# Moving the hidden chunk's send and turn behind each pair's third group, and a fast group's second ring slot ahead of its sums, in a streaming-encoder block

## The reference

```python
D_MODEL, SEQ, D_FF = 2048, 256, 5632

def rmsnorm(x, g):
    return x * rsqrt(mean(x * x, axis=-1) + EPS) * g

def swiglu(x, w_in, w_out):
    gate, up = split(x @ w_in, 2, axis=-1)      # w_in: 2048 x 11264
    return (silu(gate) * up) @ w_out            # w_out: 5632 x 2048

h = x + 0.5 * swiglu(rmsnorm(x, ffn1_norm), ffn1_w_in, ffn1_w_out)
h = h + mixer(h)
h = h + cross_attention(h, mem)
h = h + 0.5 * swiglu(rmsnorm(h, ffn2_norm), ffn2_w_in, ffn2_w_out)
out = rmsnorm(h, final_norm)
```

## Time and profile before

| | |
|---|---|
| median of 3 runs (lowest to highest) | 2130.85 us (2129.96 to 2134.89) |
| the profiled execution, and its span | 2129.56 us, 2127.5 us |
| PE busy | 2106.6 us (99%) |
| DVE busy | 1534.0 us (72%) |
| ACT busy | 1089.3 us (51%) |
| HBM traffic | 222 GB/s over the span |

### The profile page before, as it was taken

One profiled execution on the slowest core, in us unless ns is written; L12 is line 12 of the kernel. 1 busy time (PEld: TensorE's weight loads), 2 busy tenths in 40 slices (PEclk: granted clock), 3 DMA queues, 4 the chain that ended last, 5 costly groups with the idle time before them and its releaser, 6 DMA issues.

```text
span 2127.5 us, 27271 instructions
## 1 busy us (share of the span) xinstructions
PE 2106.6 (99%) x9405; PEld 1740.4 (82%) x9405; DVE 1534.0 (72%) x1647; ACT 1089.3 (51%) x1249; POOL 38.4 (2%) x50
## 2 busy tenths in 40 slices
PE   9999999999999999999999999999999999999998
PEld 7788888888888888888888888887887888888887
DVE  7999999984555576566565656569999999964444
ACT  6555555553444455456544545455555555543433
POOL 0000000000000031000000000000000000000000
PEclk9999999999999999999999999999999999999999
DMA  7676667776666676765587766575667767775554
GB/s 278 223 231 218 221 231 228 226 245 239 208 228 214 220 265 218 237 213 184 178 285 239 237 208 191 189 247 198 229 226 223 224 217 221 225 287 195 190 188 157
DMA packets 185317, 472.37 MB, mean 222 GB/s; under 512 B 17056, under 2 KB 67616, under 8 KB 185120
## 3 DMA queue, kind: packets, MB, share of 16 engines
q1 hardware_dynamic: 183088, 464.11, 66.1%
q0 software_dynamic: 1728, 6.82, 0.9%
q10 hardware_dynamic: 432, 0.53, 0.1%
HBM read 443.60 MB, written 27.79 MB: 222 GB/s over the span
## 4 chain that ended last, share of the span: by engine, by line
PE 60%; DVE 18%; DMA 11%; issue 8%; ACT 2%; DVEq 0%; SPq 0%; ACTq 0%; POOLq 0%; POOL 0%
PE acc L1869 18%; PE acc L1871 18%; PE acc L1872 18%; DMA raw<-in_ffn_w_in 11%; DVE w_lo L1186 9%; DVE t_raw L1312 2%; DVE raw L1310 2%; DVE t_raw L1309 2%; DVE stage L1293 1%; PE acc L1893 1%; PE acc L1892 1%; PE acc L1894 1%; DVE stage L1226 1%; ACT w_hi L727 1%; DVE shared L1348 0%
## 5 line engine op out<-in xcount | busy, mean ns | idle before, releaser
L1186 DVE TENSOR_TENSOR w_lo<-raw,w_hi 128x1024 fp32r<-128x1024 f32 x765 | 924.8, 1223 | 477.1 <-ACT w_hi L727 474.9
L727 ACT ACTIVATE w_hi<-raw 128x1024 fp32r<-128x1024 f32 x765 | 796.8, 1056 | 857.5 <-PE acc L1872 532.7
L1869 PE MATMUL acc<-w_hi,a_hi 128*128 128x512 f32 x744 | 290.3, 390 | 0.5 <-DVE w_lo L1186 0.5
L1872 PE MATMUL acc<-w_hi,a_lo 128*128 128x512 f32 x744 | 289.6, 389 | 0.0
L1871 PE MATMUL acc<-w_lo,a_hi 128*128 128x512 f32 x744 | 289.5, 389 | 0.0
L1869 PE MATMUL acc<-w_hi,b_hi 128*128 128x512 f32 x576 | 225.6, 392 | 0.0
L1871 PE MATMUL acc<-w_lo,b_hi 128*128 128x512 f32 x576 | 224.3, 389 | 0.0
L1872 PE MATMUL acc<-w_hi,b_lo 128*128 128x512 f32 x576 | 224.2, 389 | 0.0
L1892 PE MATMUL acc<-w_hi,a_hi 128*128 128x512 f32 x460 | 179.0, 389 | 0.0
L1893 PE MATMUL acc<-w_lo,a_hi 128*128 128x512 f32 x460 | 179.0, 389 | 0.0
L1892 PE MATMUL acc<-w_hi,b_hi 128*128 128x512 f32 x460 | 179.0, 389 | 0.0
(11 more groups left out here) (273 smaller groups left out, 2645.1 us busy)
## 6 DMA issues: line engine op xcount, KB each, us to landing
raw<-in_ffn_w_in SPq DMA_DIRECT2D x349, 512.0 KB, 4.2
raw<-in_ffn_w_out SPq DMA_DIRECT2D x176, 512.0 KB, 4.3
raw<-in_w_mix_in SPq DMA_DIRECT2D x80, 512.0 KB, 4.4
raw<-in_w_ckv SPq DMA_DIRECT2D x64, 512.0 KB, 4.3
memq<-bounce SPq DMA_DIRECT2D x196, 128.0 KB, 4.3
bounce<-stage SPq DMA_DIRECT2D x37, 512.0 KB, 3.1
raw<-in_w_mix_out SPq DMA_DIRECT2D x32, 512.0 KB, 4.5
raw<-in_w_cq SPq DMA_DIRECT2D x32, 512.0 KB, 4.3
```

Source lines behind the costliest of these rows:

```text
L727: eng.activation(w_hi[:, u % RING], raw[:, u % RING], ACT.Copy).then_inc(w_hi_done, 1)
L1186: eng.tensor_tensor(w_lo[:, u % RING], raw[:, u % RING], w_hi[:, u % RING].bitcast(f32), ALU.subtract).then_inc(w_lo_done, 1)
L1869: eng.matmul(dst, x_hi[:, rows], w_hi[:, slot, i], start=start and i == 0, stop=False)
L1872: last = eng.matmul(dst, x_lo[:, rows], w_hi[:, slot, i], start=False, stop=stop and i == UK - 1)
```

## The change

- `SEND_AT` goes from 7 to 12 and `FETCH_AT` from 10 to 14. On DVE `hidden` moves from behind place 3 to behind place 7, `turn` from behind the third group's `t_lo_part` to behind place 12, and `fill_lo` from behind place 10 to behind the first add of the gate sums. ACT's `fill_hi` moves from between places 10 and 11 to behind `copy_p1`. DVE gains a wait on its own `t_read` ahead of writing the gate to `stage`.
- TensorE does the two products of a group's second ring place ahead of the three with summed weights. The semaphore `t_used` goes: `w_used` of the second place now says that as well.
- The first pair's mixed blocks move to places 5, 7, 9 (FFN1) and 9, 11, 13 (FFN2). ACT runs a one-element Silu at place 14 (FFN1) and 6 (FFN2), so the table it needs is loaded there.

```diff
-SEND_AT = 7
-MIX_AT = [10, 12, 14][-FAST:]
-FETCH_AT = 10
+SEND_AT = 12
+FETCH_AT = 14
+X_MIX_AT = [5, 7, 9]
+H3_MIX_AT = [9, 11, 13]
...
@@ ACT, fast_hi and pair @@
                     if s:
-                        eng.wait_ge(t_used, fast_count(base, j, s))
+                        eng.wait_ge(w_used, base + PAIR * j + FAST_AT[s - 1] + 2)
...
-                        if s == FAST - 1:
-                            fill_hi(turned, number(TURNS, hid) + j, hid_dst, src=stage4)
                         split(base, j, FAST_AT[s] + 3, PAIR)
                     for p in range(4 * FAST, PAIR - 3):
                         split(base, j, p, PAIR)
                     eng.wait_ge(w_used, base + PAIR * j + FAST_END)
                     eng.activation(copy_p1, sum_p1, ACT.Copy).then_inc(p1_copied, 1)
+                    fill_hi(turned, number(TURNS, hid) + j, hid_dst, src=stage4)
...
@@ ACT, first pair (FFN1; FFN2 the same at p == 6) @@
+                    if p == 14:
+                        eng.activation(first_exp[:], ones[:, 0:1], ACT.Silu)
-                    if p - 1 in MIX_AT:
-                        s = MIX_AT.index(p - 1)
+                    if p - 1 in X_MIX_AT:
+                        s = X_MIX_AT.index(p - 1)
...
@@ DVE, pair @@
                     for s in range(FAST):
                         fast_lo(j, s)
-                        if s == FAST - 1:
-                            turn(number(TURNS, hid) - 1 + j, stage4)
                         unit_lo(j, FAST_AT[s] + 2)
                         if s == 0:
                             up_drained(j - 1)
-                        if s == FAST - 1:
-                            fill_lo(split_number(hid) - 1 + j, lo, hi, src=stage4)
                         unit_lo(j, FAST_AT[s] + 3)
-                        if s == 0:
+                        if s == 1:
                             hidden(j - 1)
                     for p in range(4 * FAST, PAIR - 3):
                         unit_lo(j, p)
+                    turn(number(TURNS, hid) - 1 + j, stage4)
                     eng.wait_ge(p1_copied, done)
                     eng.tensor_tensor(shared[:, 0], sum_p6, copy_p1, ALU.add).then_inc(p6_added, 1)
+                    fill_lo(split_number(hid) - 1 + j, lo, hi, src=stage4)
                     unit_lo(j, PAIR - 3)
...
+                    eng.wait_ge(t_read, number(FILLS, hid) + j)
                     eng.tensor_tensor(stage[:, 0], acc[:, 0], copy_p1, ALU.add)
...
@@ DVE, behind the first pair @@
-                mix_parts_lo(base, MIX_AT.index(PAIR - 2), *mixed)
...
@@ TensorE, fast @@
-                    eng.wait_ge(t_lo_done, fast_count(base, j, s) + 1)
-                    three(sum_p7, s3, sum_block(0), start, stop)
-                    three(sum_p6, s2, sum_block(1), start, stop)
-                    three(acc[:, 1], block_of(UK * s + 1, 1), sum_block(2), start, False).then_inc(t_used, 1)
-
                     eng.wait_ge(w_lo_done, unit + 2)
                     three(acc[:, 0], block_of(UK * s + 1, 0), ring_block(p + 1, 0), start, False)
                     if s == 0:
                         eng.wait_ge(up_read, silus[base] + j)
-                    three(acc[:, NT], block_of(UK * s, 1), ring_block(p + 1, 1), start, False).then_inc(w_used, 1)
+                    three(acc[:, NT], block_of(UK * s, 1), ring_block(p + 1, 1), start, False)
+
+                    eng.wait_ge(t_lo_done, fast_count(base, j, s) + 1)
+                    three(sum_p7, s3, sum_block(0), start, stop)
+                    three(sum_p6, s2, sum_block(1), start, stop)
+                    three(acc[:, 1], block_of(UK * s + 1, 1), sum_block(2), start, False).then_inc(w_used, 1)
```

More of the change, by code:

```diff
@@ L403, in encoder_block @@
         t_lo_done = sem("t_lo_done")
-        t_used = sem("t_used")
         p1_copied = sem("p1_copied")
@@ L1136, in first_pair_of_h3 @@
                         turned_h3_hi(DC - 1)
-                    if p - 1 in MIX_AT:
-                        s = MIX_AT.index(p - 1)
+                    if p == 6:
+                        eng.activation(first_exp[:], ones[:, 0:1], ACT.Silu)
+                    if p - 1 in H3_MIX_AT:
+                        s = H3_MIX_AT.index(p - 1)
                         mix_parts_hi(FFN2_IN, s, b_hi, HEAD_PAIR.index((1, s)) + 1)
@@ L1366, in ffn_in @@
                 eng.sem_inc(gate_read, 1)
-                mixed = (a_hi, a_lo) if base == FFN1_IN else (b_hi, b_lo)
-                mix_parts_lo(base, MIX_AT.index(PAIR - 2), *mixed)
                 with eng.Fori(1, DC + 1) as j:
@@ L1457, in first_pair_of_x @@
                         mean_square("x", DC, D)
[L1458 to L1462, removed]
+                    if p - 2 in X_MIX_AT:
+                        mix_parts_lo(FFN1_IN, X_MIX_AT.index(p - 2), a_hi, a_lo)
+                    if p in X_MIX_AT:
+                        mix_parts(X_MIX_AT.index(p), a_hi, a_lo)
+                    if p == 4:
                         chain(eng.memset(shared[:], 0.0))
@@ L1802, in first_pair_of_h3 @@
                                 GAIN_AT["ffn2_norm"] + 12)
[L1803 to L1807, removed]
+                    if p - 2 in H3_MIX_AT:
+                        mix_parts_lo(FFN2_IN, H3_MIX_AT.index(p - 2), b_hi, b_lo)
+                    if p in H3_MIX_AT:
+                        mix_parts(H3_MIX_AT.index(p), b_hi, b_lo)
+                    if p == 4:
                         chain(eng.memset(shared[:], 0.0))
```

## The result

The changed kernel takes 2188.32 us, median of 4 runs (2179.97 to 2190.93), against 2132.87 us (2129.96 to 2136.16, 4 runs) for the kernel before: a ratio of 1.0253, with a 95% interval of 1.0219 to 1.0287. It is slower, as forecast, and by twice what was forecast (55 us where I said 27, and above the 2176 at which my range ended). The profiled execution took 2190.51 us with a span of 2188.5, 61.0 more than the span of before.

The account below looks back on a forecast made before the run. It took PE, 99% busy, and DVE's competing loop in the FFN pairs as the bound. New stalls of 42.4 us less old ones of 14.9 gave +27.5 on 2129.56, so 2158 us at the median; range 2115 to 2176.

Parts of the forecast that it names:

- What bounds the kernel: In the FFNs' pairs: PE busy 99%, its waits 14.9 us in all; DVE's loop, with about 2 us to spare, competes.
- The loop's price of the fetch and turn: DVE's loop in FFN pairs exceeds TensorE's 41.50 us by 2.11 (FFN1) and 2.51 (FFN2): 41.6 us over nine passages each.
- F: Time from the fetch's first request to its last landing in a pair, taken as mean 7.36 us in FFN1, 7.76 in FFN2.
- the draw: Rival: gains and new stalls in the FFN pairs cancel at F of 6.03, giving 2131 us; chance 0.10.
- In the new place the company is the same: Fetch at its later place: two loads just ahead, two just behind, as before, so the old mean F was kept.
- in time: Rival: F below 5.25 at the new place, DVE's loop shorter than TensorE's, 2117.5 us; chance 0.16.
- The send: Rival: the send in the pairs lands late and pushes the fetch back 1.6 us, 29 us more, 2187; chance 0.08.
- FFN1's first pause: At FFN1's start, DVE's lead of 5.4 us falls 1.5 short of the 6.92 wanted: a 1.5 us stall.
- 36.25 + F: DVE's whole loop in us, from one pair's first sums to the next pair's, exceeding TensorE's 41.50 by F - 5.25.
- it comes out of the next stall, as DVE sets the pace, and I add nothing: After new 2 us stalls of PE the lower granted clock may return, worth 1.7 us before; priced at nothing.
- TensorE's reordering: In TensorE's groups: the same 21 matmuls in a new order, claimed to cost nothing.
- DVE waits elsewhere in the pair: Sign of being wrong: DVE waiting elsewhere in the pair would mean the loop of 36.25 + F leaves something out.

Follow-up runs that it names:

- change_up_read_last: The changed kernel with the product that needs `up_read` moved behind the sums, last in its group: 2148.85 us, ratio 1.0093 to the kernel before.
- pause_filled: The changed kernel with six useless matmuls more in each pair, ahead of the wait for `up_read`: 2172.62 us, ratio 1.0198 to the kernel before.
- up_read_last: The changed kernel with the fetch ahead of place 13's load, not 14's, and the `up_read` product last in its group: 2110.94 us, 0.9918 of before.
- fetch_early: The changed kernel with `hidden` back behind place 3, the send at place 7 and the fetch at place 12: 2140.65 us, ratio 1.0060 to before.

## Why the prediction was right in sign and wrong in size

*What bounds the kernel* was right: PE's pauses in the pairs, and DVE's loop behind them. The old pauses were 16 us rather than 14.9, and 1.6 more for the clock.

*The loop's price of the fetch and turn* was right. F was forecast at 7.36 and 7.76 and came to 7.9 and 7.3; the turns waited 3.06 us each; the part behind the turn took the 10.27 forecast. change_up_read_last, where DVE's waits for `w_hi` are gone from the pairs, costs what this term gives. By the Trainium skill's formula ("DMA: Bandwidth & Descriptors", "Anatomy of one DMA") F would be 3.8 by estimate and the turn never late. It was rightly set aside: that section fits it to transfers issued by GpSimd, these are issued by SP, and the quickest mean of F in any run was 4.7 (up_read_last, FFN2), the quickest single one 3.95. One reading was wrong: "none of the 20 in pairs was under 6.4". The pair whose fetch went out at 1510.58 had its last request land after 4.5 us, F = 6.0, so the draw had a little more for it than I said.

*"In the new place the company is the same"* was right for this place and hid the lever. F depends on how many loads are under way when the fetch begins: 7.5 us with two, 5.1 with one. The rivals "in time" and "a draw" are reached by one line of the schedule, and I had priced F as given.

*The send* was in time everywhere; that rival fell. Its figure, 2187, lies near the result for another reason.

*FFN1's first pause* was 2.83 us (matmul starts) against 1.5 forecast.

*The step that failed* is the loop itself, 36.25 + F, taken as DVE's alone: "it comes out of the next stall, as DVE sets the pace, and I add nothing", and TensorE's reordering at "nothing". The reordering put a wait at PE's ninth matmul in place of the eighteenth. With the sums late, the pause there is passed on through `w_used` and ACT's `w_hi` to DVE at places 5 and 7, inside the very loop that set the pause. I had added up DVE's instructions and its one new wait, and had not asked of the others (for `w_hi`) what the new pause of PE does to them. They grew by 29.8 us; 13.9 of that is there at full clock as well (7.7 + 8.2 in pause_filled, less 2.0). The lower clock, priced at nothing, was worth about 12 us of the time. That DVE waits elsewhere in the pair is the sign of being wrong that I had named. In the profiled spans the sum is 27.5 forecast + 29.8 for these waits (part of what the lower clock costs shows in them) + 1.3 for FFN1's first pause - 2.7 for the larger old stalls = 55.9 of 61.0; 5 us are not placed. (The medians lie 55 apart, since the profiled execution of after is 2 us above its median and that of before 3 below.)

The rows of before carried the warning. By the earlier trace rows DVE comes to place 7 at 10.01 + 4.93 + 1.67 + 1.14 = 17.75 us after the sums, and with the pause at the ninth matmul PE and ACT can serve it at 8.96 + 8.16 + 1.0 = 18.1. I had all the terms and did not make the sum.

What stays open: why 12 of the 20 pauses (2.4 to 2.9 us between starts) were followed by the lower clock and 8 not, though six of the 8 were as long, 2.2 to 2.9 us. No run was made on it.

## What to carry to other kernels

When an engine is late and another pauses for it, follow the pause once round the ring: if it delays the release of a buffer that the late engine needs, both wait in turn, and the loop is longer than either engine's sum. Halves of a change that cost 0 and 21 us cost 55 together, so cut a change in two before explaining it. And before pricing a transfer from its old duration, count the loads that will still be under way ahead of it, and look at which load stands directly behind: moving it by one entry was worth 2.9% here.

## What was not expected of the hardware

- Four requests of 128 KB took 7.5 us in the mean from the first request to the last landing with two 512 KB loads of the same queue under way, and 5.1 with one, even where that one had been issued only 0.5 to 0.7 us before (5.2 to 5.75, three cases). The load behind the fetch landed after 6.3 us in fetch_early.
- The granted clock fell to 0.50 after 12 of TensorE's 20 pauses, all 12 of 2.4 to 2.9 us, for about 3.4 us each time (in one case twice that), at 1.6 us a time. In the run with idle matmuls, whose longest pause was 1.6 us between starts, it did not fall.
